# TensorE's expert loop in a decoder block: its body of three expert pairs runs over pairs 1 to 14 in place of pairs 4 to 12

## What is computed

```python
logits = (hf @ router_w + router_b).astype(jnp.float32)
top_logits, top_idx = lax.top_k(logits, TOP_K)          # 4 of 32
gates = jax.nn.softmax(top_logits, axis=-1).astype(h.dtype)
...
def expert_block(args):
    xb, e = args
    gu = xb @ w_gate_up[e] + b_gate_up[e]               # 1024 -> 2048
    gate, up = gu[..., :D_FF_EXPERT], gu[..., D_FF_EXPERT:]
    gate = jnp.minimum(gate, SWIGLU_LIMIT)
    up = jnp.clip(up, -SWIGLU_LIMIT, SWIGLU_LIMIT)
    act = (up + 1.0) * gate * jax.nn.sigmoid(SWIGLU_ALPHA * gate)
    return act @ w_down[e] + b_down[e]                  # 1024 -> 1024
```

## Time and profile before

| | |
|---|---|
| median of 3 runs | 1188.1 us (1187.67 to 1188.52) |
| the profiled execution | 1185.88 us, its span 1184.2 us |
| PE busy | 1106.1 us, 93% of the span |
| DMA, mean over the span | 368 GB/s |
| DMA, from 285 us to 1157 us | 427 to 432 GB/s, a share of 1.00 to 1.01 |
| mean granted TensorE clock | 0.982 |

### The profile page before, as it was taken

How to read it: one execution, slowest core, us unless ns; L and a number is a source line. 1 busy time by engine, 2 the same in 40 slices (tenths; PEclk the granted TensorE clock), 3 DMA queues, 4 the chain that set the end, 5 groups by cost and what they waited for, 6 DMA issues and landing times.

```text
span 1184.2 us, 13896 instructions
## 1 busy us (share of the span) xinstructions
PE 1106.1 (93%) x5819; PEld 532.7 (45%) x5819; DVE 350.5 (30%) x740; ACT 166.9 (14%) x272; POOL 4.0 (0%) x23
## 2 busy tenths in 40 slices
PE   7999999999999999999898989898989898989897
PEld 6889886764434333433333333333334333333332
DVE  4685234463313212212121212222222213121313
ACT  3431234441101000010101010101010101010002
POOL 1000000000000000000000000000000000000000
PEclk9999999999999999999999999999989899999999
DMA  9842314677999999999999999999999999999995
GB/s 341 301 143 72 143 71 116 273 279 301 428 429 426 428 427 434 428 431 428 432 427 432 429 430 431 429 433 428 431 432 432 427 436 427 431 428 436 424 428 215
DMA packets 39029, 435.65 MB, mean 368 GB/s; under 512 B 5813, under 2 KB 5898, under 8 KB 20330
## 3 DMA queue, kind: packets, MB, share of 16 engines
q1 hardware_dynamic: 37066, 433.67, 87.2%
q10 hardware_dynamic: 1920, 1.34, 0.6%
HBM read 433.95 MB, written 1.05 MB: 367 GB/s over the span
## 4 chain that ended last, share of the span: by engine, by line
PE 58%; DMA 39%; DVE 1%; ACT 1%; issue 1%; SPq 0%; DVEq 0%; PEldq 0%
DMA ring<-in_w_down 35%; PE ps L2037 18%; PE ps L1997 14%; PE ps L1560 4%; PE ps L1671 4%; PE ps L1617 3%; DMA ring<-in_w_gate_up 3%; PE ps L2052 3%; PE ps L1540 2%; PE ps L1667 2%; PE ps L1728 2%; PE ps L1966 2%; PE ps L1804 1%; PE ps L1848 1%; DMA ring<-in_w_in 1%
## 5 line engine op out<-in xcount | busy, mean ns | idle before, releaser
L2037 PE MATMUL ps<-ring,work 128*64 128x512 f32 x1024 | 247.4, 633 | 38.6 <-DMA ring<-in_w_down 35.6
L1997 PE MATMUL ps<-ring,work 128*64 128x512 f32 x1024 | 225.6, 593 | 9.2 <-DMA ring<-in_w_gate_up 9.2
L1997 PE MATMUL ps<-work 128*64 128x512 f32 x1024 | 230.4, 592 | 0.2 <-DVE work L1396 0.2
L2037 PEld LDWEIGHTS ps<-ring,work 128*64 128x64 f32 x1024 | 81.0, 145 | 179.8 <-issue 163.4
L1997 PEld LDWEIGHTS ps<-ring,work 128*64 128x64 f32 x1024 | 71.2, 137 | 159.1 <-issue 140.7
L1997 PEld LDWEIGHTS ps<-work 128*64 128x64 f32 x1024 | 71.5, 137 | 136.7 <-issue 129.6
L1416 DVE TENSOR_SCALAR work<-ps 128x512 f32<-128x512 f32 x32 | 22.0, 686 | 197.7 <-PE ps L1540 197.7
L1439 DVE COPY work<-ps 128x512 f32<-128x512 f32 x16 | 11.1, 692 | 223.4 <-PE ps L1540 223.4
L1451 DVE COPY work<-ps 128x512 f32<-128x512 f32 (+1 forms) x16 | 11.1, 691 | 222.3 <-PE ps L2037 222.3
L2052 PE MATMUL ps<-work 128*128 128x512 f32 (+1 forms) x132 | 59.7, 608 | 10.4 <-ACT work L796 10.2
L1540 PEld LDWEIGHTS ps<-small,work 128*128 128x128 f32 (+1 forms) x354 | 44.8, 170 | 51.4 <-issue 45.4
(11 more groups left out here) (240 smaller groups left out, 728.3 us busy)
## 6 DMA issues: line engine op xcount, KB each, us to landing
work<-in_w_gate_up SPq DMA_DIRECT2D x64, 2048.0 KB, 36.5
ring<-in_w_gate_up SPq DMA_DIRECT2D x24, 4096.0 KB, 32.2
ring<-in_w_down SPq DMA_DIRECT2D x22, 4096.0 KB, 35.9
ring<-in_w_down SPq DMA_DIRECT2D x19, 2048.0 KB, 21.6
ring<-in_w_gate_up SPq DMA_DIRECT2D x16, 2048.0 KB, 20.2
ring<-in_w_in SPq DMA_DIRECT2D x7, 2048.0 KB, 15.9
ring<-in_xattn_w_kv SPq DMA_DIRECT2D x2, 2048.0 KB, 13.9
ring<-in_w_out SPq DMA_DIRECT2D x2, 2048.0 KB, 8.1
```

Source lines behind the costliest of these rows:

```text
L1997: last = nc.tensor.matmul(bank(b)[p], xg_T[k][:, kb, :], quad_columns(w[:, kk, D_MODEL * (q // 2):D_MODEL * (q // 2 + 1)], q % 2), start=F ...
L2037: last = nc.tensor.matmul(bank(Y_BANK + y)[p], act_T[k][:, b, HALF * c:HALF * c + HALF], w[:, b, 512 * q:512 * q + 512], start=False, stop ...
```

## The change

TensorE's loop now begins with pair 1 and has five turns, pairs 1 to 3, 4 to 6, 7 to 9, 10 to 12 and 13 to 14. In the last turn the third pair is skipped by a branch (`pe.If`). Pair 0 stands ahead of the loop and pair 15 behind it. Since the body now also serves pairs 1 to 3, it waits for the second places as well. Their counts are reached in pair 3 at the latest and don't go up any more in the first pass, so there the register is left out (`kind_of_place` 2). Which products TensorE does, with what operands and in what order, stays as it was. No other engine's instructions change.

```diff
+            def kind_of_place(s):
+                return 1 if s >= RING else 2 if s in [second for _, second in TWIN_PLACES] else 0
+
             def chunk_landed(s, loads, turned16):
                 if loads is not None:
-                    pe.wait_ge(S(f"slot_loaded{s}"), turned16[s >= RING] + 16 * (loads + 1))
+                    pe.wait_ge(S(f"slot_loaded{s}"), turned16[kind_of_place(s)] + 16 * (loads + 1))
                 return place(s)
...
-                for i in range(BY_HALVES):
-                    pair_of_experts(0, i, i, 2 * i + 1, 2 * i + 2, lambda c: first_pass_chunk(i, c), (0, 0),
-                                    opening=None if i else lambda: second_gather(0))
-                with pe.Fori(0, TURNS) as rev:
-                    turned16 = pe.snap(rev * (16 * TURN_USES)), pe.snap(rev * (16 * TURN_PAIRS))
-                    for q in range(BY_HALVES, BY_HALVES + TURN_PAIRS):
+                pair_of_experts(0, 0, 0, 1, 2, lambda c: first_pass_chunk(0, c), (0, 0, 0),
+                                opening=lambda: second_gather(0))
+                whole_turns = (PAIRS - 1) // TURN_PAIRS
+                with pe.Fori(0, whole_turns) as rev:
+                    turned16 = pe.snap(rev * (16 * TURN_USES)), pe.snap(rev * (16 * TURN_PAIRS)), 0
+
+                    def one_of_turn(q):
                         i = pe.snap(rev * TURN_PAIRS + q)
                         pair_of_experts(0, i, i, pe.snap(2 * i + 1), pe.snap(2 * i + 2),
                                         lambda c: first_pass_chunk(q, c), turned16)
-                for i in range(PAIRS - TURN_PAIRS, PAIRS):
-                    pair_of_experts(0, i, i, 2 * i + 1, 2 * i + 2, lambda c: first_pass_chunk(i, c), (0, 0),
-                                    final=(i == PAIRS - 1), pieces=(i == PAIRS - 1))
+
+                    one_of_turn(1)
+                    one_of_turn(2)
+                    with pe.If(rev < whole_turns - 1):
+                        one_of_turn(3)
+                i = PAIRS - 1
+                pair_of_experts(0, i, i, 2 * i + 1, 2 * i + 2, lambda c: first_pass_chunk(i, c), (0, 0, 0),
+                                final=True, pieces=True)
```

More of the change, by code:

```diff
@@ L2125, in first_pass, with later_turned16 @@
                                         lambda c: first_pass_chunk(q, c), turned16)
-                for i in range(PAIRS - TURN_PAIRS, PAIRS):
-                    pair_of_experts(0, i, i, 2 * i + 1, 2 * i + 2, lambda c: first_pass_chunk(i, c), (0, 0),
-                                    final=(i == PAIRS - 1), pieces=(i == PAIRS - 1))
+                    one_of_turn(1)
[5 more added lines that the diff above has]
+                                final=True, pieces=True)
+            def later_turned16(done, i):
+                loads16 = pe.snap(done * 32 + 32 * i)
+                return loads16, 0, loads16
             def later_pass(r):
@@ L2135, in later_pass @@
                     pair_of_experts(r, i, pe.snap(r * PAIRS + i), pe.snap(r * E + 2 * i + 1),
-                                    pe.snap(r * E + 2 * i + 2), later_pass_chunk, (pe.snap(done * 32 + 32 * i), 0))
+                                    pe.snap(r * E + 2 * i + 2), later_pass_chunk, later_turned16(done, i))
                 i = PAIRS - 1
                 pair_of_experts(r, i, pe.snap(r * PAIRS + i), pe.snap(r * E + 2 * i + 1), pe.snap(r * E + 2 * i + 2),
-                                later_pass_chunk, (pe.snap(done * 32 + 32 * i), 0), final=True)
+                                later_pass_chunk, later_turned16(done, i), final=True)
             pe.sem_inc(S("act_T_filled"), 1)
```

## The result

The changed kernel takes 1192.2 us in the median of six runs (1190.9 to 1194.3), the kernel before 1187.0 us (1185.9 to 1188.5). The ratio is 1.0047, with an interval of 1.0037 to 1.0056: slower, by some 5.6 us. The forecast was no change, 1188.1 us, and a range up to 1190.2. The profiled execution of the changed kernel is the slowest of its six: 1194.3 us, span 1192.6.

A forecast was written before the change was run, and what follows sets the result against it. The full weight stream (427 to 430 GB/s from 285 us) was taken to set the end. Stream, array, tail and jump to pair 15 each added 0, so the forecast was the median, 1188.1 us, range 1186.4 to 1190.2.

The forecast's parts named there:

- The two regimes of TensorE: Pairs 1 to 3 run at TensorE's own pace, 52.9 us each; from pair 4 it waits for the stream, later pairs 58 to 59.
- the slack of 4.0 us a pair: TensorE's waits for weights in pairs 4 to 14, 43.5 us together, taken as time it can lose there.
- the end as a landing plus a fixed tail: Pair 15: the full stream's chunk lands at 1144.77 us, then 31.6 us of products and a short tail.
- Rival B: Jump to pair 15 misses its instructions and the clock falls too: slower, 1190.8 to 1191.6 us; chance 0.06.
- taken skip to pair 15: The last turn's `pe.If` branch over the third pair: 0.21 to 0.235 us on the sequencer, 0 on the array.
- added waits: 44 waits for second places in pairs 4 to 14, 0 to 2.2 us; register waits in pairs 1 to 3, 0 to 1.8.
- first step: Loop body's instruction packets come in pairs 1 to 3, none in pairs 4 to 14, then some for pair 15.
- Two signs that I had named as wrong: Profile signs that would refute the forecast: a branch of 3 us, and instruction packets in every turn.
- Rival C: Every turn back misses: nine to twelve us of stalls in four places, inside the slack, time still 1188.1 us; chance 0.05.
- the price of a miss: A jump to instructions not at hand, at a pair's start: 2.3 to 3.1 us on the array, from a 3.30 us branch.
- Bandwidth: Weight stream: five pairs fewer of instruction packets, 0.19 MB less, at most 0.4 us gained, kept as the lower bound.
- E: Faster by over 0.2%: needs a higher stream rate or another clock; fewer packets give 0.4 us at most; chance 0.05.

The follow-up runs named there:

- the one with fewer bytes: Changed kernel, each weight load from pair 4 on bringing a quarter of its bytes, for its trace alone: 1146.6 us, one execution.
- changed, slot 0, held up 44: Changed kernel, loop starting at a 256-instruction fetch block's first place, plus 44 empty sequencer passes after pairs 3, 6, 9 and 12: ratio 1.0117.
- changed, hint: Changed kernel with a prefetch hint for the loop's branch back as first instruction of each turn: ratio 1.0002.
- changed, slot 0: Changed kernel with its loop's first instruction at slot 0 of a 256-instruction fetch block (one 16 KB packet): ratio 0.9984.
- changed, slot 0, held up 18: Changed kernel, loop starting at a 256-instruction fetch block's first place, plus 18 empty sequencer passes after pairs 3, 6, 9 and 12: ratio 0.9986.
- changed, slot 104: Changed kernel with its loop's first instruction at slot 104 of a 256-instruction fetch block: 1184.5 us, one execution.
- before, slot 0: Kernel before the change, with only its loop's first instruction moved to slot 0 of a 256-instruction fetch block: ratio 1.0005.
- written out: TensorE's 16 pairs all written out, with no loop and no branch, against the kernel before: ratio 1.0026.
- before, slot 160: Kernel before the change, with only its loop's first instruction moved to slot 160 of a 256-instruction fetch block: ratio 1.0025.
- changed, slot 128: Changed kernel with its loop's first instruction at slot 128 of a 256-instruction fetch block: 1194.1 us, one execution.

## Why the prediction was wrong, point by point

**Right.** The two regimes of TensorE, the full stream, the slack of 4.0 us a pair and the end as a landing plus a fixed tail held in every kernel but the one that was held up too long (and the one with fewer bytes). Landing and end of the profiled executions, sorted by packets in the stream:

| kernel | packets | spread, us | landing to end, us | ratio |
|---|---|---|---|---|
| changed, slot 0, held up 44 | 9 | 2.9 | 45.2 | 1.0117 |
| changed, hint | 9 | 3.3 | 39.4 | 1.0002 |
| changed, slot 0 | 10 | 3.7 | 39.4 | 0.9984 |
| changed, slot 0, held up 18 | 10 | 3.4 | 39.4 | 0.9986 |
| changed, slot 104 | 10 | 3.5 | 39.4 | 1184.5 us, once |
| before | 20 | 5.5 | 39.4 | 1 |
| before, slot 0 | 21 | 5.9 | 39.4 | 1.0005 |
| written out | 33 | 8.2 | 39.4 | 1.0026 |
| before, slot 160 | 39 | 8.4 | 39.5 | 1.0025 |
| changed | 42 | 11.1 | 39.9 | 1.0047 |
| changed, slot 128 | 43 | 11.4 | 39.9 | 1194.1 us, once |

Rival B's 1.7 us for a lower clock is the 5.35 us less the 3.65 of the earlier trace rows; the granted clock there was 0.50 from 574.8 to 578.2 us. In the first part of the changed kernel's pair 15 it was 1.00.

The costs of the taken skip to pair 15 (0.24 us), of the `pe.If` (0.08) and of the added waits (nothing to be seen: pairs 1 to 3 at 52.9 to 53.0 us) came as predicted.

**Wrong, first step:** "So a body of three pairs, once fetched, stayed at hand ... I expect its packets in pairs 1 to 3, none in pairs 4 to 14". I took a property of one place for one of the body. Before, the body of 1674 instructions happened to lie where it stayed at hand. With its 6 instructions more (the traces record 1678 a turn against 1674) it still stays at slots 0 and 104 (turns back of 0.2 us, 10 packets). But removing three pairs ahead of it moved it by some six and a half blocks (an estimate, three pairs being about 1674 instructions), and where it came to lie it doesn't stay. Two signs that I had named as wrong came with it, a branch of 3 us and more and instruction packets in every turn. The order of the instructions, which I had read, doesn't show this. Rival C, every turn back misses, had 0.05.

How many blocks stay at hand no run counts out. Without a hint, the seven that the loop touches at slots 0 and 104 did, and the eight that it touches at slots 128 and 160 did not (turns back of 6.9 to 7.3 us with 43 packets, and of 6.2 to 6.4 us with 39).

**Second:** the price of a miss, 2.3 to 3.1 us on the array. It was 25.4 us in four places, 6.4 on average. The row I took it from, a jump of 3.30 us at the end, has no weight stream beside it. That alone would not have changed the time, as the run with 18 passes shows.

**Third, and this is the 5.6 us:** "Bandwidth: ... 0.19 MB less, 0.4 us of the stream at most". That step priced instruction packets by dividing their bytes by the rate of 16 engines. For the 22 packets more of the changed kernel that gives 22 x 16 KB = 0.36 MB, 0.8 us. The spread grew by 5.7 us, 0.26 us a packet; for the 13 more of the kernel written out by 2.7 us, 0.21 each; for the 19 more of the kernel before at slot 160 by 3.0 us, 0.16 each; for the 10 fewer at slot 0 it shrank by 1.7 us. The ratios say the same: 1.0047, 1.0026, 1.0025 and 0.9984 of 1187 us are +5.6, +3.1, +3.0 and -1.9 us. A weight load is whole when its last mark is there (in the kernel written out the last one is at 1149.3 us, and the product that had waited 1.99 us for the load starts at 1149.38), and eight of the 16 carry the burden (in the changed kernel the ninth mark comes 6.0 us behind the eighth, at 1149.3 and 1143.3 us). The stairs in the marks say how: each packet falls on one engine. Added up over all 16 marks, the lag grows by 1.2 to 1.7 us a packet of 16 KB in the ten kernels whose stream stays full, and an eighth of that, 0.15 to 0.21 us, is about what a packet adds to the spread (0.26 in the changed kernel is more). So a packet costs its engine two to three times the 0.6 us that 16 KB take at an engine's 27 GB/s (an estimate, the measured 430 over 16), and with eight engines hit and not 16 this doubles. With it fell the premise "Something moves the end only if it empties the stream, or delays TensorE in pair 15 by more than the 1.3 us that it waits there": here the stream's share stayed at 1.00, and the lag of its last engine moved the end by 5.7 us. For the same reason C was wrong to say that the trace would differ and the time not, and E to put fewer packets at 0.4 us.

What stays open: why a packet costs its engine 1.2 to 1.7 us and not 0.6; why eight engines are hit; and the hint's run, whose spread (3.3) would let one expect 0.998 and which measured 1.0002, its interval just meeting that of slot 0.

## What to carry to other kernels

Where the transfers are the bound, as here, a program's instruction packets are traffic too (0.15 to 0.26 us of spread each), and they are to be priced at the engines that carry them, not as a share of all bytes. Read the instruction queue's packets by stretch, and the 16 marks of a landing one by one. A long loop that turns back fast in one program may miss in the next because of where it lies (here 0.2 us at slot 0 and 7.1 us in the changed kernel as it was): pin it to a slot of a block, or give the turn a hint (both 0.2 us here), before judging any change of the code around it. Here the change with its loop at slot 0 takes 0.9984 (0.9974 to 0.9994) of before, and no kernel that was run several times is clearly faster.

## What the hardware showed unexpectedly

Each instruction packet of 16 KB sets one DMA engine back by 1.2 to 1.7 us while the weight stream is full, and eight of the 16 fall behind the other eight in this way: in the changed kernel by 6 us from the eighth engine to the ninth, and 11 us from first to last, while the mean share of all 16 stays at 1.00. A stall of 6 us with 6.8 us at half clock (granted 0.50) behind it, four times over, costs nothing (0.9986 against 0.9984 without), although TensorE is 93% busy by the page.
